# Two heads at a time in the second layer's attention, and a feed-forward's second product by Strassen's scheme

## The chip, the cores and the metric

The kernel runs on one core of one Trainium2 chip. The metric is the device time of one execution in microseconds; each version is run several times and the median is given. A separate, profiled execution gives the trace: for each instruction its engine, start, duration and what released it. Engine names in the rows: PE is TensorE's matrix multiply, PEld its weight load, DVE is VectorE, ACT is ScalarE, POOL is GpSimd and SP is SyncE, which only issues the DMAs here. All data is f32.

## The reference, cut to what matters

Two transformer blocks follow each other on 256 tokens of width 1024. The first (gated linear attention, retention and a mixture of 32 experts) is not touched. The second has a mixer of two attentions, then a cross-attention to a memory, then a feed-forward. What the change touches:

```
# mixer: 8 DSA heads and 8 NSA heads of width 64, 256 tokens, causal
idx = sum_h relu(q_i[h] @ k_i.T) * w_i[h]           # 8 index heads -> which 64 keys each query keeps
o_dsa[h] = softmax(q_d[h] @ k_d.T on the 64 kept keys) @ v_d            # one k, v for all 8 heads
o_cmp[h] = softmax(q_n[h] @ k_c[g].T) @ v_c[g]      # 15 compressed keys, g = h // 4
o_slc[h] = softmax(q_n[h] @ k_slc[g].T) @ v_slc[g]
o_win[h] = softmax(q_n[h] @ k_win[g].T) @ v_win[g]
o_nsa[h] = o_cmp * gate[h, 0] + o_slc * gate[h, 1] + o_win * gate[h, 2]
x = x + concat(o_dsa, o_nsa) @ w_out
...
x = x + square(relu(rms_norm(x) @ w_ff_in)) @ w_ff_out      # 1024 -> 4096 -> 1024
```

With 256 tokens the selection of blocks and the window reach over all earlier keys, so that both are plain causal attention here. The kernel thus has 24 attentions of one head (8 selected, 8 window, 8 DSA), and the eight small ones on 15 compressed keys.

## The kernel before

One program per engine, written out by hand; the engines meet at semaphores that count upwards, and each engine does its instructions in the order written. SyncE streams the weights as tiles of 1 MB through a ring of six (`RING`); a tile's slot is loaded again when the matmuls that read it have signalled. PSUM has eight banks of 128x512 f32. Banks 0 to 3 take the planned sums (`SUMS`, handed out in turn by `fresh`, taken by ScalarE with `take` or `copy`); banks 4 to 7 are used by hand. Queries are held turned (features by tokens) and two heads to a tile of 128 rows: the even head in rows 0 to 63, the odd one in 64 to 127; the keys stand doubled in both halves. `RT(q)` is such a pair tile.

The stage around the change, in TensorE's order:

- Index scores: for each of eight heads `causal_scores` (lines 1660 and 1661) into bank 4 or 5. It makes two matmuls, queries 0 to 127 against keys 0 to 127, and queries 128 to 255 against all 256 keys, 384 columns in all. ScalarE takes the relu (line 1032), VectorE adds it up with the head's weight (line 2411).
- Compressed scores (line 1675) for both halves, first all even heads, then all odd ones. VectorE masks them, ScalarE takes the exponential, VectorE sums. TensorE transposes the result (line 1684, `cp0` to `cp3`) and multiplies by the compressed values (line 1690, `co0`, `co1`). ScalarE copies the two banks out, VectorE divides by the sum and multiplies by the gate (line 2444) and so begins `OA`, the output by tokens.
- The loop over 24 heads. In turn n TensorE makes the scores of head n (one of banks 4 and 5), the three transposes of the probabilities of head n-2 (line 1718, banks 6 and 7), and the value product of head n-3 (lines 1729 to 1731), in which the turned probabilities are the weights and the 64 columns of V move. VectorE adds the mask (line 2477) and takes the two maxima (line 2487). In the first 16 turns it also does one step of the search for the 64 best keys, eight at a time on one row tile (lines 2483 and 2493). ScalarE takes the exponentials with their sums (line 1053), copies the turned probabilities (line 1062), and after each four heads copies the output bank (line 1070). VectorE's `finish` then divides by the sums, multiplies by the gate and adds into `OA` (lines 2454 to 2466).
- After the loop `OA` is transposed (`aT0` to `aT3`, line 1188) into `oT2`, and the output projection `ao0` to `ao3` runs (line 1179).

The feed-forward at the end: 16 tiles `ff0` to `ff15` (line 1170) with relu by ScalarE and the square by VectorE (line 2557), giving `ffh`, 32 blocks of 128 features by 256 tokens. Then 16 tiles of 256 x 1024 weights: for each, two row tiles of tokens, two halves of 512 output columns and two blocks of 128 features, 128 matmuls of 512 columns in all (line 1822), added up in banks 4 to 7. When the first two banks are complete (`tile0_done`) VectorE adds them to the residual with a factor per token (line 2562); the other two follow at the end, and SyncE stores the output by row tile (line 566).

## Time and profile before

| | |
|---|---|
| median of 3 runs | 1346.31 us (1344.46 to 1349.18) |
| profiled execution | 1351.78 us, with a span of 1350.0 us from first to last instruction |
| TensorE busy (matmul) | 1277.1 us, 95% of the span |
| VectorE busy | 289.7 us, 21% |
| ScalarE busy | 334.2 us, 25% |
| mean granted TensorE clock | 0.938 of full speed |
| feed-forward's second half | 110.0 us of matmul busy time on line 1822 |

The busy shares are of the whole span; stages differ, and the rows further down are read by stage. A record of the trace is one instruction. An f32 matmul and its weight load appear as two records each, a transpose as one. The duration of a matmul record includes the time in which it is in the pipeline together with the next, so that the cost of one matmul in a series is the distance from start to start. In a merged row (x8) the time runs from the first start to the last end. The granted clock has two levels, 1.00 (2.4 GHz) and 0.50 (1.2 GHz); a value between them is a stretch with both.

### The profile page before, as it was taken

How to read it: one execution, taken by the hardware profiler on the slowest of the kernel's cores; microseconds unless marked ns; L12 is line 12 of the kernel's file. 1: busy time of each engine (PE TensorE's matmuls, PEld its weight loads, DVE VectorE, ACT ScalarE, POOL GpSimd, SP SyncE). 2: the span in 40 equal slices, each digit the busy share in tenths (PEclk: the TensorE clock that was granted, in tenths of full speed). 3: DMA queues.
4: the chain of work that ended last, by engine and by line, in shares of the span. 5: the costliest groups of instructions: out<-in, count | busy, mean ns of one | idle time of the engine just before them, and what ended most of it. 6: DMA issues, size and time to landing. Idle time of an engine off the chain costs nothing.

```text
span 1350.0 us, 16638 instructions
## 1 busy us (share of the span) xinstructions
PE 1277.1 (95%) x6964; PEld 958.0 (71%) x6964; DVE 289.7 (21%) x757; ACT 334.2 (25%) x728; POOL 20.3 (2%) x26
## 2 busy tenths in 40 slices
PE   6899999999999899999999998967999979999998
PEld 5688888888887688865555556756677857887443
DVE  1200000012322211311111112683552121000000
ACT  3375100053322400321112213223333241000000
POOL 0000000000000000000000001020000000000000
PEclk9999999999999899899999999985555989999999
DMA  9921122213256954569999965430000413444430
GB/s 365 415 96 63 65 92 94 94 63 121 98 218 254 372 184 147 212 248 408 420 418 424 420 276 219 152 103 28 1 0 1 132 56 127 154 156 156 156 125 31
DMA packets 34362, 241.66 MB, mean 179 GB/s; under 512 B 3898, under 2 KB 4282, under 8 KB 6012
## 3 DMA queue, kind: packets, MB, share of 16 engines
q1 hardware_dynamic: 32640, 233.85, 45.1%
q10 hardware_dynamic: 1020, 4.02, 0.8%
q0 software_dynamic: 640, 2.90, 0.6%
q8 instruction: 46, 0.75, 0.2%
q14 instruction: 16, 0.13, 0.0%
HBM read 239.71 MB, written 1.05 MB: 178 GB/s over the span
## 4 chain that ended last, share of the span: by engine, by line
PE 88%; DVE 6%; ACT 2%; DMA 2%; issue 1%; SPq 0%; DVEq 0%; ACTq 0%
PE bank L1179 21%; PE bank L1170 20%; PE bank L1531 8%; PE bank L1822 8%; PE bank L1554 4%; PE bank L1493 3%; PE bank L1502 2%; DMA ring<-in_stream 2%; PE bank L1209 2%; PE bank L1661 1%; PE bank L1660 1%; PE bank L1229 1%; PE bank L1796 1%; PE bank L1406 1%; PE bank L1351 1%
## 5 line engine op out<-in xcount | busy, mean ns | idle before, releaser
L1170 PE MATMUL bank<-arena,ring 128*128 128x256 f32 x736 | 159.3, 379 | 0.0
L1170 PEld LDWEIGHTS bank<-arena,ring 128*128 128x128 f32 x736 | 139.8, 190 | 19.0
L623 ACT ACTIVATE arena<-bank 128x512 f32<-128x512 f32 x96 | 56.8, 597 | 340.1 <-PE bank L1170 211.3
L1179 PE MATMUL bank<-ring,arena 128*128 128x256 f32 x544 | 123.0, 387 | 7.3 <-DMA ring<-in_stream 4.4
L1179 PEld LDWEIGHTS bank<-ring,arena 128*128 128x128 f32 x544 | 105.0, 194 | 23.0 <-DMA ring<-in_stream 4.9
L1179 PE MATMUL bank<-ring,hTl 128*128 128x256 f32 x512 | 113.4, 380 | 0.0
L1170 PE MATMUL bank<-hTl,ring 128*128 128x256 f32 x512 | 112.6, 379 | 0.0
L1822 PE MATMUL bank<-ring,arena 128*128 128x512 f32 x256 | 110.0, 592 | 0.0
L1170 PEld LDWEIGHTS bank<-hTl,ring 128*128 128x128 f32 x512 | 97.0, 190 | 16.1 <-issue 3.4
L1179 PEld LDWEIGHTS bank<-ring,hTl 128*128 128x128 f32 x512 | 96.9, 190 | 15.2 <-issue 2.3
L1822 PEld LDWEIGHTS bank<-ring,arena 128*128 128x128 f32 x256 | 48.6, 190 | 60.8 <-issue 60.7
L1179 PE MATMUL bank<-ring,hTc 128*128 128x256 f32 x384 | 84.8, 379 | 0.0
L1179 PEld LDWEIGHTS bank<-ring,hTc 128*128 128x128 f32 x384 | 72.9, 190 | 11.7 <-issue 1.9
L1531 PE MATMUL bank<-ring,arena 128*64 128x256 f32 x512 | 57.0, 381 | 0.0
L1531 PEld LDWEIGHTS bank<-ring,arena 128*64 128x64 f32 x512 | 36.1, 137 | 24.0 <-issue 6.7
L2209 DVE TENSOR_TENSOR arena<-bank,arena 128x512 f32<-128x512 f32 x32 | 22.1, 692 | 101.9 <-PE bank L1554 101.9
L926 ACT ACTIVATE arena<-bank 128x256 f32<-128x256 f32 x16 | 6.1, 384 | 151.7 <-PE bank L1531 151.7
L912 ACT ACTIVATE arena<-bank,mod 128x256 f32<-128x256 f32 x72 | 36.5, 561 | 19.8 <-PE bank L1493 19.8
L1493 PE MATMUL bank<-arena 128*128 128x128 f32 x288 | 39.5, 281 | 1.4 <-DVE arena L2173 1.2
L1493 PEld LDWEIGHTS bank<-arena 128*128 128x128 f32 x288 | 34.8, 191 | 7.9 <-issue 7.5
L1502 PE MATMUL bank<-arena 64*128 64x512 f32 x136 | 33.8, 615 | 0.8 <-DVE arena L2209 0.8
L1053 ACT ACTIVATE arena<-arena,smx 128x128 f32<-128x128 f32 (+1 forms) x48 | 21.4, 447 | 52.4 <-DVE smx L2487 36.6
(445 smaller groups left out, 1462.6 us busy)
## 6 DMA issues: line engine op xcount, KB each, us to landing
ring<-in_stream SPq DMA_DIRECT2D x163, 1024.0 KB, 5.4
arena<-in_stream SPq DMA_DIRECT2D x38, 1024.0 KB, 9.1
hTl<-in_stream SPq DMA_DIRECT2D x9, 1024.0 KB, 8.2
hTc<-in_stream SPq DMA_DIRECT2D x9, 1024.0 KB, 10.1
consts<-in_consts ACTq DMA_DIRECT2D x1, 2665.0 KB, 13.3
arena<-in_mem SPq DMA_DIRECT2D x1, 1024.0 KB, 8.3
arena<-in_x SPq DMA_DIRECT2D x1, 1024.0 KB, 23.9
arena<-in_ctx SPq DMA_DIRECT2D x1, 1024.0 KB, 27.2
```

Of the source, the lines that this page charges most:

```text
L623: act.activation(dst, b[:, :].rearrange("p (a b) -> p a b", b=two), func, scale=scale).then_inc(sum_taken, 1)
L912: ins = act.activation(xgs[q][:, k, :].rearrange("p (e j c) -> p j e c", e=4, j=NT), b[:, 256 * m:256 * m + 256].rearrange("p (j e c) -> p ...
L1053: act.activation(sS[n % 3][:, a:z], sS[n % 3][:, a:z], ACT.Exp, bias=smx[:, 2 * (n % 4) + i:2 * (n % 4) + i + 1], accum_out=sm[:, i, hh:hh ...
L1170: mm = pe.matmul(b[:, 256 * n:256 * n + 256], w[:, k, 128 * n:128 * n + 128], h[:, k, :], start=(k == 0), stop=(k == KD - 1))
L1179: mm = pe.matmul(b[:, 256 * i:256 * i + 256], h[:, k, 128 * i:128 * i + 128], w[:, k, :], start=(k == 0), stop=(k == KD - 1))
L1209: mm = pe.matmul(b[:, 256 * i:256 * i + 256], h[:, k, 128 * i:128 * i + 128], w[:, k, :], start=(k == 0 and i == 0), stop=(k == KD - 1), s ...
L1493: mm = pe.matmul(bank[1 + fill % 2][:, at:at + 128], xn2[:, j, 128 * k:128 * k + 128], Pm[:, j, :], start=True, stop=True)
L1502: mm = pe.matmul(acc[2 * j + n][:, :], hT_PT[own, 256:384], ysb[own, 512 * n:512 * n + 512], start=False, stop=False, skip_group_check=True)
L1531: mm = pe.matmul(bank[0][CAP * e:CAP * e + CAP, FF * a:FF * a + FF], xgs[q][:, k, at:at + CAP], w[e][:, k, :], start=(k == 0), stop=(k == ...
L1554: mm = pe.matmul(bank[1 + m][to:to + CT, :], hT_PT[:, of:of + CT], wd[e][:, k, 512 * m:512 * m + 512], start=(k == 0), stop=(k == 1), skip ...
L1822: mm = pe.matmul(acc[2 * j + n][:, :], ffh[:, 2 * q + k, 128 * j:128 * j + 128], w[:, k, 512 * n:512 * n + 512], start=(q == 0 and k == 0) ...
L2209: dve.tensor_tensor(ysb[:, 512 * m:512 * m + 512], bank[1 + m][:, :], g2bc[:, 512 * m:512 * m + 512], ALU.mult).then_inc(R.y_taken, 1)
```

## The change

**Attention, two heads in a step.** The 24 turns become 12 steps (`STEPS`): eight for the NSA heads (`pair_step` alternates the selected and the window attention of one pair), four for the DSA pairs.

- `pair_of_scores` issues the two heads' matmuls alternately, even head from rows 0 to 63 into one bank, odd head from rows 64 to 127 into the next. The index scores use it too.
- VectorE adds the mask and takes the negated maximum in one `tensor_tensor_reduce` per head and row tile, four in a step. It does both row tiles' top-8 search and replacement in each of the first eight steps. It scales the probabilities by one over their sum and by the gate (`pair_norm`) before they are transposed; `finish` and `OA` are gone.
- The value product is turned round: V (keys by 64) is the weight, and the turned probabilities move, 256 columns for the first key block and 128 for the second. The even head writes partitions 0 to 63 of a bank, the odd one 64 to 127. Selected, window and compressed parts are added up in the same bank, and the result is `oT2` as it stands; four copies by ScalarE take it out. The transposes `aT0` to `aT3` and the sums `co0`, `co1` are gone.
- The compressed scores come ahead of the index scores and alternate the row halves; their softmax runs among the index heads and scales before the transposes. The product with the compressed values is eight matmuls in column tiles at step 2.

**Feed-forward's end by Strassen.** Each tile of 256 x 1024 weights is read as a 2x2 matrix of blocks (128 features by 512 columns), the activations likewise (128 features by 128 tokens). Seven products per tile, each with a bank of its own over all 16 tiles, take the place of eight. VectorE makes the sums of the activations (`fsum`, after each square) and of the weights (`wsum`, two buffers). At the end the seven banks go into the four quarters of the residual in twelve updates (`contribute`).

The core of the diff:

```diff
-            for h in range(H2):
-                if h >= 2:
-                    pe.wait_ge(idx_relu, h - 1)
-                causal_scores(bank[4 + h % 2], 8 + h // 2, 17, h % 2).then_inc(idx_ready, 1)
+            def pair_of_scores(at, qpair, kpair, ready):
+                for i, (a, z) in enumerate(TILES):
+                    for half in range(2):
+                        r = slice(64 * half, 64 * half + 64)
+                        mm = pe.matmul(bank[at + half][:, a:z], RT(qpair)[r, 128 * i:128 * i + 128],
+                                       RT(kpair)[r, 0:z - a], start=True, stop=True)
+                        if i == 1:
+                            mm.then_inc(ready, 1)
...
+            for p in range(4):
+                if p == 1:
+                    pe.wait_ge(cs_sub, 1)
+                elif p >= 2:
+                    pe.wait_ge(idx_relu, 2 * p - 2)
+                pair_of_scores(4 + 2 * (p % 2), 8 + p, 17, idx_ready)
+            pe.wait_ge(cs_norm, 1)
...
+            for s in range(STEPS + 3):
+                if s < STEPS:
+                    q, k, _ = pair_step(s)
+                    if s >= 2:
+                        pe.wait_ge(s_max, s - 1)
+                    else:
+                        pe.wait_ge(idx_relu, 6 + 2 * s)
+                    pair_of_scores(4 + 2 * (s % 2), q, k, s_ready)
+                if s == 2:
+                    pe.wait_ge(sum_taken, NO["cp3"] + 1)
+                    for p in range(4):
+                        for half in range(2):
+                            h = 2 * p + half
+                            pe.matmul(bank[p // 2][64 * half:64 * half + 64, 256 * (p % 2):256 * (p % 2) + 256],
+                                      VC[0:NCMP, p // 2, :], PCT[0:NCMP, 2 * h:2 * h + 2, :],
+                                      start=(p % 2 == 0), stop=False, skip_group_check=True)
+                m = s - 2
+                if 0 <= m < STEPS:
+                    pe.wait_ge(pair_norm, m + 1)
+                    for half in range(2):
+                        if m >= 1:
+                            pe.wait_ge(pt_taken, 2 * m + half - 1)
+                        for c in range(3):
+                            mm = pe.transpose(bank[2 + half][:, 128 * c:128 * c + 128], sS[m % 3][:, half, 128 * c:128 * c + 128], ident)
+                        mm.then_inc(pt_ready, 1)
+                m = s - 3
...
-                    mm = pe.matmul(b[:, HD * hh:HD * hh + HD], T[:, 0:128], v(0), start=True, stop=True)
-                    pe.matmul(b[:, 256 + HD * hh:256 + HD * hh + HD], T[:, 128:256], v(0), start=True, stop=False)
-                    mm = pe.matmul(b[:, 256 + HD * hh:256 + HD * hh + HD], T[:, 256:384], v(1), start=False, stop=True)
-                    mm.then_inc(av_done, 1)
-            pe.wait_ge(o_taken, 7)
-            for k in range(4):
-                turn(f"aT{k}", OA, k)
+                    for k in range(2):
+                        for half in range(2):
+                            last = k == 1 and (m % 2 == 1 or m >= H2)
+                            mm = pe.matmul(b[64 * half:64 * half + 64, at + 128 * k:at + 256], v(k),
+                                           pT[m % 2][:, half, 256 * k:256 * k + 256 - 128 * k],
+                                           start=(m in (8, 10) and k == 0), stop=last, skip_group_check=True)
...
-                S(dve.tensor_tensor(sS[n % 3], bank[4 + n % 2][:, 0:384], mask, ALU.add))
...
-                for i, (a, z) in enumerate(((0, 128), (128, 384))):
-                    dve.tensor_reduce(smx[:, 2 * (n % 4) + i:2 * (n % 4) + i + 1], sS[n % 3][:, a:z], AX.X, ALU.max,
-                                      negate=True).then_inc((dve_step, s_max)[i], 1)
...
+                    for half in range(2):
+                        for i, (a, z) in enumerate(TILES):
+                            ins = dve.tensor_tensor_reduce(sS[s % 3][:, half, a:z], bank[4 + 2 * (s % 2) + half][:, a:z], mask[:, a:z],
+                                                           -1.0, 3e38, ALU.add, ALU.min,
+                                                           nmax[:, s % 2, 2 * half + i:2 * half + i + 1])
+                    ins.then_inc(s_max, 1)
...
+                m = s - 1
+                if m >= 0:
+                    dve.wait_ge(probs, m + 1)
+                    W(dve.reciprocal(pair_sum[:, m % 2, :], pair_sum[:, m % 2, :]))
+                    for half in range(2):
+                        for i, (a, z) in enumerate(TILES):
+                            r = pair_sum[:, m % 2, 2 * half + i:2 * half + i + 1]
+                            pr = sS[m % 3][:, half, a:z]
+                            if m < H2:
+                                h = 2 * (m // 2) + half
+                                ins = dve.tensor_scalar(pr, pr, r, gates[:, i, h, 1 + m % 2:2 + m % 2], ALU.mult, ALU.mult)
+                            else:
+                                ins = dve.tensor_scalar(pr, pr, r, None, ALU.mult)
+                    ins.then_inc(pair_norm, 1)
...
-                for j in range(NT):
-                    for n in range(2):
-                        for k in range(2):
-                            mm = pe.matmul(acc[2 * j + n][:, :], ffh[:, 2 * q + k, 128 * j:128 * j + 128],
-                                           w[:, k, 512 * n:512 * n + 512], start=(q == 0 and k == 0), stop=(q == 15 and k == 1))
+                pe.wait_ge(fsum_ready, q + 1)
+                product(2, rows_sum[:, 128:256], w[:, 0, 0:512])
+                product(5, rows_sum[:, 0:128], w[:, 1, 512:1024])
+                if q == 0:
+                    pe.wait_ge(sum_taken, len(SUMS))
+                pe.wait_ge(wsum_ready, q + 1)
+                product(3, f0[:, 0:128], w3)
+                product(4, f1[:, 128:256], w4)
+                product(1, diag, w1)
+                product(7, across, w67[:, 1, :])
+                mm = pe.matmul(prod[6][:, :], down, w67[:, 0, :], start=(q == 0), stop=(q == 15))
                 mm.then_inc(ffo_done, 1)
...
+            def weight_sums(q):
...
+                if q >= 2:
+                    dve.wait_ge(ffo_done, q - 1)
+                dve.tensor_tensor(w3, w[:, 0, 512:1024], w[:, 1, 512:1024], ALU.subtract)
+                dve.tensor_tensor(w4, w[:, 1, 0:512], w[:, 0, 0:512], ALU.subtract)
+                dve.tensor_tensor(w1, w[:, 0, 0:512], w[:, 1, 512:1024], ALU.add)
+                dve.tensor_tensor(w67, w[:, :, 0:512], w[:, :, 512:1024], ALU.add).then_inc(wsum_ready, 1)
```

## Rows read from the trace of the kernel before

**Rows 1.** The page: clock over 40 slices of the span, and the chain by engine.

```profile
PEclk9999999999999899899999999985555989999999
...
PE 88%; DVE 6%; ACT 2%; DMA 2%; issue 1%; SPq 0%; DVEq 0%; ACTq 0%
```

**Rows 2.** Stretches: start and end, length, busy PE, PEld, DVE, ACT, POOL, clock, DMA.

```profile
945.00:1037.00 92.00, 85.63 (x309) 65.38 (x308) 48.32 (x154) 35.73 (x126) 0.00 (x0) 0.50 0.00 1
...
1235.00:1346.00 111.00, 110.52 (x260) 48.87 (x258) 2.54 (x4) 0.60 (x1) 0.00 (x0) 1.00 0.30 109
```

**Rows 3.** Timeline of one head: start us, us, engine, line, operation.

```profile
976.40 0.79 PE L1660 MATMUL bank<-hTc,hTl 64*128 64x128 f32 x2
...
977.98 0.90 PE L1718 MATMUL bank<-consts,arena 128*128 128x128 f32 x3
978.08 0.56 DVE L2477 TENSOR_TENSOR arena<-bank,consts 128x384 f32<-128x384 f32 x1 [2.82 <-PE bank L1661]
...
978.67 0.52 PE L1729 MATMUL bank<-arena 128*128 128x64 f32 x2
...
978.88 0.61 DVE L2487 TENSOR_REDUCE smx<-arena 128x1 f32<-128x128 f32 x2
...
979.98 0.79 PE L1660 MATMUL bank<-hTc,hTl 64*128 64x128 f32 x2
```

**Rows 4.** Timeline of the loop's start, heads 0 and 1 together.

```profile
944.18 0.81 PE L1660 MATMUL bank<-hTc,hTl 64*128 64x128 f32 x4 [0.69 <-ACT arena L1043]
...
945.86 0.56 DVE L2477 TENSOR_TENSOR arena<-bank,consts 128x384 f32<-128x384 f32 x1 [0.63 <-PE bank L1661]
```

**Rows 5.** Timeline of the experts' stage, TensorE, where matmuls use parts of the array.

```profile
652.28 3.64 PE L1554 MATMUL bank<-arena 128*32 128x512 f32 x32
655.85 7.13 PE L1531 MATMUL bank<-ring,arena 128*64 128x256 f32 x64
...
664.00 1.99 PE L1502 MATMUL bank<-arena 64*128 64x512 f32 x8
```

**Rows 6.** Groups of instructions by shape: count, busy us, mean ns of one, idle before.

```profile
L2557 DVE TENSOR_TENSOR arena<-arena 128x512 f32<-128x512 f32 x16 | 11.1, 693 | 94.8 <-ACT arena L623 94.8
...
L1053 ACT ACTIVATION_READ_ACCUMULATOR arena<-arena,smx 128x1 f32 x48 | 9.0, 187 | 0.0
...
L2483 DVE MAX8 top<-arena 128x8 f32<-128x256 f32 x8 | 3.3, 417 | 0.0
...
L2493 DVE MATCH_REPLACE8 arena<-top,arena 128x256 f32<-128x256 f32 x8 | 3.3, 409 | 0.0
...
L2009 DVE TENSOR_SCALAR arena<-arena,hv 128x256 f32<-128x256 f32 x8 | 2.8, 348 | 0.0
...
L2282 DVE TENSOR_SCALAR arena<-arena,mv,hms 128x64 f32<-128x64 f32 x2 | 0.6, 312 | 0.0
```

**Rows 7.** Timeline ahead of the loop: index scores, compressed scores and their product.

```profile
916.02 0.50 PE L1660 MATMUL bank<-arena,hTc 64*128 64x128 f32 x4
...
922.98 6.33 PEld L1675 LDWEIGHTS bank<-arena,hTl 64*128 64x128 f32 x32
...
936.41 7.09 PE L1690 MATMUL bank<-arena 15*128 15x64 f32 x32 [0.68 <-ACT arena L1038]
```

**Rows 8.** After the loop: timeline, then stretches with busy PE, clock and DMA.

```profile
1036.92 3.47 PE L1188 MATMUL bank<-consts,arena 128*128 128x128 f32 x16 [1.91 <-DVE arena L2466]
...
1041.07 11.28 PE L1179 MATMUL bank<-ring,arena 128*128 128x256 f32 x51 [0.69 <-ACT arena L623]
...
1039.00:1040.00 1.00, 1.00 (x7) 0.50 0.00 0
1040.00:1041.00 1.00, 0.39 (x3) 0.98 0.00 0
```

**Rows 9.** The feed-forward's second half: its group on the page, and its last updates.

```profile
L1822 PE MATMUL bank<-ring,arena 128*128 128x512 f32 x256 | 110.0, 592 | 0.0
...
1345.56 1.41 DVE L2562 SCALAR_TENSOR_TENSOR arena<-bank,r,arena 128x512 f32<-128x512 f32 x2 [2.02 <-PE bank L1822]
```

More of the change, by code:

```diff
@@ L217, in plan @@
     sums.extend(f"cp{n}" for n in range(4))
-    sums.extend(["co0", "co1"])
-    sums.extend(f"aT{k}" for k in range(4))
     for j in range(4):
@@ L2402, in _, with idx_added @@
             dve.wait_ge(kc_ready, 1)
-            for h in range(H2):
+            dve.wait_ge(heads_ready, 4)
+            dve.wait_ge(cs_ready, 2)
+            c16 = cS.rearrange("p (g n) -> p g n", n=16)[:, :, 0:NCMP]
+            cm = C("cmask").rearrange("p (i n) -> p i n", i=NT)
+            for par in range(2):
+                for i in range(NT):
+                    at = 8 * par + 4 * i
+                    S(dve.tensor_tensor(c16[:, at:at + 4, :],
+                                        bank[6 + par][:, 64 * i:64 * i + 64].rearrange("p (h n) -> p h n", n=16)[:, :, 0:NCMP],
+                                        cm[:, i, :].unsqueeze(1).broadcast_to([P, 4, NCMP]), ALU.add))
+                    step.one()
+            dve.wait_ge(dve_step, step.n)
+            W(dve.tensor_reduce(cmx, c16, AX.X, ALU.max))
+            W(dve.tensor_scalar(cmx, cmx, -BIG / 10, None, ALU.max))
+            dve.tensor_tensor(c16, c16, cmx.unsqueeze(2).broadcast_to([P, 16, NCMP]), ALU.subtract).then_inc(cs_sub, 1)
+            def idx_added(h):
                 dve.wait_ge(idx_relu, h + 1)
-                for i, (a, z) in enumerate(((0, 128), (128, 384))):
+                for i, (a, z) in enumerate(TILES):
                     w = wsc[:, i, h:h + 1]
@@ L2417, in _ @@
                         dve.wait_ge(idx_taken, h + 1)
[L2418 to L2432 removed]
+            for h in range(2):
+                idx_added(h)
             dve.wait_ge(cs_exp, 1)
@@ new lines, in _ @@
+                S(dve.tensor_tensor(c4[:, par, :, :], c4[:, par, :, :], gates[:, :, par:8:2, 0], ALU.mult))
+                step.one()
+            dve.wait_ge(dve_step, step.n)
+            dve.tensor_tensor(c16, c16, crs.unsqueeze(2).broadcast_to([P, 16, NCMP]), ALU.mult).then_inc(cs_norm, 1)
+            for h in range(2, H2):
+                idx_added(h)
+            W(dve.tensor_tensor(iacc, iacc, C("causal"), ALU.add))
+            for s in range(STEPS + 1):
+                if s < STEPS:
+                    dve.wait_ge(s_ready, 2 * s + 2)
+                    if s >= 3:
+                        dve.wait_ge(pt_ready, 2 * s - 4)
+                    mask = C("causal") if s < H2 else ibias
+                    for half in range(2):
+                        for i, (a, z) in enumerate(TILES):
+                            ins = dve.tensor_tensor_reduce(sS[s % 3][:, half, a:z], bank[4 + 2 * (s % 2) + half][:, a:z], mask[:, a:z],
+                                                           -1.0, 3e38, ALU.add, ALU.min,
+                                                           nmax[:, s % 2, 2 * half + i:2 * half + i + 1])
+                    ins.then_inc(s_max, 1)
+                if s < H2:
+                    for i, (a, z) in enumerate(TILES):
+                        S(dve.max(top8[:, 8 * i:8 * i + 8], iacc[:, a:z]))
+                        step.one()
+                    dve.wait_ge(dve_step, step.n)
+                    for i, (a, z) in enumerate(TILES):
+                        S(dve.match_replace(iacc[:, a:z], top8[:, 8 * i:8 * i + 8], iacc[:, a:z], -3e38))
+                        step.one()
+                    dve.wait_ge(dve_step, step.n)
+                if s == H2 - 1:
```

309 lines of the change are left out of this document (131 added, 178 removed).

## The prediction, made before the changed kernel was run

> **What bounds the kernel now.** I read the page's second part and its chain first. The chain that ends last is 88% TensorE, so a microsecond of TensorE work on it is a microsecond of time, and the clock row has one long trough, at 5 of 10 (the lower level, 1.2 GHz, against 2.4), between slices 27 and 31 [rows 1]. The table of stretches puts the trough on the attention: from 945 to 1037 us TensorE is busy 85.6 of 92 us, VectorE 48.3, ScalarE 35.7, and the granted clock is 0.50 throughout. The second half of the feed-forward (from 1235) is at 1.00, with VectorE almost idle (2.5 of 111 us) [rows 2]. So both edited stages are bound by TensorE, the first at the lower clock, and each has idle VectorE time to spend.
>
> The attention's period is read from one head: its score matmuls start at 976.40 and the next head's at 979.98, so 3.58 us for a head [rows 3]. An f32 matmul is two records. At this clock a 256-column one takes 0.85 us and a 128-column one 0.43: 1.28 for the scores. Three transposes are 0.64 (977.98 to 978.67, with a 0.05 handover). The three value matmuls stream only 64 columns each but load 128 columns of weights twice, six loads at 0.21, 1.28. These are 3.20; the other 0.38 is the two changes between the 64-row and the 128-row array shape, each about 0.2. Twenty-four heads are 86 us.
>
> **The change, part by part.** Times below are positions in the span of the profiled run.
>
> *Scores in row tiles.* The trace of before already holds the case by accident. One head's scores, issued at 976.40, reach VectorE at 978.08, 1.68 us later [rows 3]. Heads 0 and 1, which stand in different halves of the rows and in different banks, are issued together at 944.18, all eight records have started by the time VectorE starts on them at 945.86, again 1.68 us [rows 4]. The MoE's row-tiled L1502 agrees: eight 512-column records in 1.99 us, where one at a time would be 8 x 0.43 = 3.4 [rows 5]. So two heads' scores cost 1.28 us, not 2.56.
>
> *Value product turned round, in column tiles.* V (64 columns) becomes the weights and the probabilities move: per head one matmul of 256 columns and one of 128, 1.28 us at this clock; two heads use the two column halves. The MoE runs just this shape: L1531, 128x64 weights and 256 columns, 64 records in 7.13 us, 0.11 each, where L1822's rate (512 columns in 0.43) gives 0.215 for one alone; and four 32-column tiles (L1554) are four times as fast [rows 5, 9]. I take full overlap: 1.28 for two heads, the upper bound being 2.56. The six transposes stay, 1.28. The array changes shape three times in a step (rows, full, columns), 0.57.
>
> Here the Trainium skill speaks against the change: "TensorEngine Tiling (Array Packing)", section Tiling Modes, says that a change of tiling mode drains TensorE. The trace agrees, as the 0.38 us per head above; by rule and row alike the three changes are in my sum already.
>
> TensorE's step of two heads is then 1.28 + 1.28 + 1.28 + 0.57 = 4.4 us at the lower clock, against 7.16 before.
>
> *VectorE's step* becomes nearly as long. Before, per head: mask add 0.56, two maxima 0.61 together [rows 3]. Now four tensor_tensor_reduce do both, of 128 and 256 columns from two banks. No row shows one; the nearest is a tensor_tensor (0.69 for 512 columns, 0.56 for 384, so about 0.21 and 0.34 from start to start): 1.2 us. If each also needs a separate read of its accumulator, as ScalarE's 0.19 us ones, it is 2.0 [rows 6]; below 1.2 it can't go, as every column still passes once. In the first eight steps both top-8 searches and replacements follow (0.42 and 0.41 for 256 columns, some two thirds of that for 128; 1.5 us with their loads and waits). The division by the sum, formerly on the finished output, now scales the probabilities: a reciprocal and four tensor_scalar with one or two scalars per row, between 0.31 (two scalars, 64 columns) and 0.35 (one scalar, 256 columns) each, with waits 1.5 us [rows 6]. Together 4.3 us (upper bound 5.3) for steps 0 to 7, 2.8 to 3.6 for 8 to 11. ScalarE was busy 35.7 us for 24 heads less three [rows 2], some 1.5 a head, and does the same work in a step for two: 3.0.
>
> How they interlock: transposes of step s-2 wait for VectorE's scaling at the end of its step s-1; then TensorE goes through transposes, values and the scores of s+1 (4.5 us with handovers) before VectorE can begin s+1. The two overlap except for that 4.5, so I take 4.6 for steps 0 to 7 and 4.4 after.
>
> *Ahead of the loop.* Before: index scores from 916.0, block scores to 929.6 (L1675, 32 records at 0.2, weight-load bound), softmax, transposes, L1690 (sixteen matmuls, 7.1 us, no cover), first head scores at 944.18 [rows 7, 4]. Now the block scores come first and alternate row halves (3.2 to 6.3 us; I take 4.5, as no row shows two 128-column loads in different halves by themselves): done by 920.5. The softmax chain on VectorE runs beside the index pairs; cs_norm comes at about 926, the transposes end at 929.5, VectorE, the last in this part, adds index heads 2 to 7 (0.8 each with waits, an estimate from the 0.56 of one 384-column operation) until 931.5 and starts step 0 there. TensorE already has its scores. L1690 becomes eight column-tiled matmuls of 256 columns (3.4 us) that TensorE runs at step 2 while it waits for the first scaling (at 939): covered; without that cover they cost 3.4.
>
> *The loop.* Step 0 (no scaling) ends 934.2; seven at 4.6: 966.4; the index bias, 1.0: 967.4. Then TensorE sets the end: scores 9 finished at 971.9, two more steps 980.7, and the drain (three groups of transposes, four of values, one copy) 11.3: the output projection starts at 992.0. Before it was 1041.07 [rows 8]. What also goes: the last division and the sixteen turning transposes, since the product comes out already turned. Attention: 49.1 us less.
>
> *Clock after it.* Before, the clock rose at about 1040, after the transposes of L1188 had run back to back since 1036.92, so the projection began at 1.00 [rows 8]. Now it may begin at 0.50: some 4 us of it at half speed cost 2. Add 2.0.
>
> *Feed-forward by Strassen.* Per 256x1024 weight tile seven 512-column products instead of eight. 128 matmuls have 256 records at 0.43, 0.857 us for one [rows 9]; sixteen go: -13.7. VectorE makes the sums of the weights: per tile five 512-column adds, 5 x 0.69 = 3.5 us at most, beside 6.0 us of TensorE; with two buffers this stays hidden (without cover it would cost up to 3.5 x 16 = 56). The activation sums, some 1.3 us per tile, stand beside the first half's 6.9 us per tile (16 matmuls of 0.43). The first weight sum is made before the last tile of the first half; the second is ready 5.7 us after it, and needed at 7.7.
>
> The end grows. Before, VectorE has two updates after the last matmul, 1345.56 to 1346.97 [rows 9]. Now twelve updates of 0.7 follow seven products; the first can start 5.1 us before the last product ends, so they end 3.5 us behind it instead of 1.6: +1.9, and the first half of the output leaves almost with the second instead of 3.4 us ahead: +0.9. Together +2.8.
>
> **Sum.** -49.1 + 2.0 - 13.7 + 2.8 = -58.0 us. Against the profiled run's 1351.78 that is 1293.8. The median of the runs shown, 1346.31, is 5.5 lower; the same difference off it gives **1288.3**.
>
> **The rivals.** (a) *The clock rises inside the loop.* For: a step now holds more streaming per microsecond (3.84 of 4.6 us against 2.56 of 3.58), and the clock has risen upon transposes alone [rows 8]. Against: it stayed at 0.50 through a stage in which TensorE was 93% busy [rows 2]. The first eight steps, then bound by VectorE's 4.3, hardly gain; the last four fall from 4.4 to about 3.2 and the drain halves: 7 to 8 us, and the 2.0 goes: 1279. The Trainium skill, "TensorE: Matmul & The Clock Gate", section Part 4: PE-mode transpose, says that transposes don't count as activity for the clock. By that rule the step would have 2.56 us of activity in 4.6, less than before, and this rival falls. The trace disagrees: only transposes ran before 1040. (b) *VectorE sets the step*: the fused operation needs its accumulator read, 5.3 to 5.5 us for steps 0 to 7 and some wait in the others: +7 to +10, 1297. (c) *The tiles don't overlap or Strassen is not covered*: value products one after the other, +1.28 x 12 = 15; or the seven products wait for sums. Against: rows 5. About 1304. (d) *Slower than before*: the fused reduction in VectorE is so dear that it eats all. The other savings are worth some 58 us, so a step would have to take 58/12 = 4.8 us more, 9.4 in all, which is 6.3 for four instructions, 1.6 each, over four times the nearest row. Above that the kernel is slower, 1355 for 1.7 us each. (e) *It doesn't do what it says*: nothing in the diff leaves the old loop in place, so this is in (c).
>
> **Chances.** Forecast 0.42, (a) 0.27, (b) 0.18, (c) 0.10, (d) 0.02, 0.01 left. The forecast's own range is 1283 to 1294 (block scores, handovers, the bound of the copies). With (a) and (b): 1276 to 1302. 0.3% is about what a measurement of this kernel can tell from no change: faster 0.97, same 0.01, slower 0.02.
>
> **What the profile would show.** Right: the output projection (L1179's arena records) starts near 992; start to start of pair scores 4.6 us in the first eight steps, 4.4 in the last four; the score records of both halves in pairs; the feed-forward's second half 112 matmuls in 96 us; seven products 6.0 us apart; 3.5 us of VectorE after the last. Wrong: tensor_tensor_reduce rows over 0.45 us or with a second record (b); a granted clock of 1.00 between 931 and 990 (a); value records at 0.43 each for 256 columns (c); idle TensorE between products, released by VectorE's weight sums (c).

## The result and the profile after

The changed kernel takes 1276.93 us (median of 4 runs, 1275.76 to 1280.01) against 1346.32, a ratio of 0.9486 with a 95% interval of 0.9462 to 0.9511: 69.4 us less, where 58.0 were forecast. The time lies at the lower end of the range given (1276 to 1302) and outside the forecast's own 1283 to 1294. It is nearest to rival (a), 1279, and 11.4 us below the forecast of 1288.3.

The page of the changed kernel: the clock row and the chain, as in [rows 1].

```profile
PEclk9999999999999999999999999899778989999999
...
PE 85%; DVE 7%; ACT 2%; DMA 2%; SPq 2%; issue 1%; DVEq 0%; ACTq 0%
```

The long trough of 5s is gone. Two slices at 7 are left where the attention now stands.

The two profiled runs differ by 76.0 us of span (1350.0 and 1274.0), more than the medians. In four pieces:

| piece | before | after | difference | forecast |
|---|---|---|---|---|
| up to the compressed keys (L1652, now L1665) | 915.8 | 910.8 | -5.0 | 0 |
| from there to the output projection (L1179, now L1192) | 125.3 | 65.9 | -59.4 | -49.1 |
| from there to the last product's first matmul | 194.4 | 194.3 | -0.1 | +2.0 |
| feed-forward's second half to the span's end | 114.5 | 103.0 | -11.5 | -10.9 |

The first piece has no edit in it. Over the fourteen profiled runs of this document it lies between 910.6 and 915.8 us, so its 5.0 us are scatter, with the profile of before at the top (its 1351.78 against a median of 1346.31 said so already). The edits are worth 71 us in the profiles. Of the attention's 59.4, 16.4 are saved ahead of the loop (30.1 to 13.7 us) and 43.0 from its start to the output projection (95.2 to 52.2).

Timeline of the changed kernel from the compressed keys to the loop (start us, us, engine, line, operation), to be held against [rows 7]. CUSTOM_DVE_ANT_0 is how the trace names the tensor_tensor_reduce:

```profile
910.84 0.29 PE L1665 MATMUL bank<-consts,arena 15*128 15x15 f32 x2 [2.35 <-DVE ss L2426]
911.50 1.74 PE L1687 MATMUL bank<-arena,hTl 64*128 64x15 f32 x22 [0.38 <-ACT arena L1042]
...
914.09 1.68 PE L1675 MATMUL bank<-arena,hTc 64*128 64x128 f32 x8
...
919.87 1.92 PE L1703 MATMUL bank<-consts,arena 128*15 128x128 f32 x16
...
924.53 0.29 DVE L2485 CUSTOM_DVE_ANT_0 arena<-bank,consts 128x128 f32<-128x128 f32 x1
...
927.15 3.67 PE L1718 MATMUL bank<-arena 15*64 15x256 f32 x16
```

The loop's first VectorE instruction comes 13.7 us after the compressed keys; before it was 30.1 (915.8 to 945.86 in [rows 4]). The compressed scores (L1687) are through in 2.6 us, where [rows 7] have 6.3. While the clock is at 0.50, two of their records, one in each row half, take 0.21 us together; before, each took 0.21.

Timeline of one step at each clock, the lower first:

```profile
935.07 1.54 PE L1728 MATMUL bank<-consts,arena 128*128 128x128 f32 x6 [0.79 <-DVE arena L2511]
...
936.54 1.55 PE L1742 MATMUL bank<-arena 128*64 128x256 f32 x8
...
938.02 1.65 PE L1675 MATMUL bank<-hTc,hTl 64*128 64x128 f32 x8
...
939.75 0.29 DVE L2485 CUSTOM_DVE_ANT_0 arena<-bank,consts 128x128 f32<-128x128 f32 x1 [0.81 <-PE bank L1675]
...
947.59 0.28 DVE L2485 CUSTOM_DVE_ANT_0 arena<-bank,consts 128x128 f32<-128x128 f32 x1
947.73 0.88 PE L1728 MATMUL bank<-consts,arena 128*128 128x128 f32 x6 [1.39 <-DVE arena L2511]
...
948.36 0.42 DVE L2485 CUSTOM_DVE_ANT_0 arena<-bank,consts 128x256 f32<-128x256 f32 x1
948.54 0.87 PE L1742 MATMUL bank<-arena 128*64 128x256 f32 x8
948.70 0.08 DVE L2485 DVE_READ_ACCUMULATOR2_ANT arena<- 128x1 f32 x1
948.70 0.61 DVE L2491 MAX8 top<-arena 128x8 f32<-128x128 f32 x2
...
949.34 0.93 PE L1675 MATMUL bank<-arena,hTl 64*128 64x128 f32 x8
...
950.13 0.18 DVE L2504 RECIPROCAL arena<-arena 128x4 f32<-128x4 f32 x1
950.35 1.25 DVE L2511 TENSOR_SCALAR arena<-arena 128x128 f32<-128x128 f32 x4
...
951.51 0.28 DVE L2485 CUSTOM_DVE_ANT_0 arena<-bank,consts 128x128 f32<-128x128 f32 x1
```

At 0.50 the six transposes, the four value matmuls and the four score matmuls start 1.47 and 1.48 us apart, and VectorE gets the scores 1.73 us after their start: 4.7 us, and VectorE waits 0.81 for them. At 1.00 the same three take 2.5 us, TensorE stands idle 1.39 us until VectorE has scaled the probabilities, and VectorE doesn't wait at all: its own 3.92 us (947.59 to 951.51) are the period. The reducing instruction costs what a tensor_tensor does (0.42 us for 256 columns out of a bank, as line 2206 of the kernel before: 0.421); its accumulator read is a record of 0.08 us within the distance to the next.

Stretches of the changed kernel: start and end, length, busy PE, clock, DMA.

```profile
939.90:956.00 16.10, 9.86 (x88) 1.00 0.00 0
956.90:960.40 3.50, 3.50 (x21) 0.53 0.00 0
960.70:970.00 9.30, 6.58 (x58) 1.00 0.01 2
970.70:973.70 3.00, 3.00 (x15) 0.50 0.00 0
```

The clock is low from 926 to 939.7, high for most of what follows, and falls twice, each time after TensorE had stood idle (2.38 us before 956.6, 2.04 us before 970.5). That a gap of this length always brings a fall is not shown: `one_buffer`, further down, has the same attention code and a gap of 2.05 us at the second place, and there the clock stayed at 1.00. The end of the feed-forward, as in [rows 9]:

```profile
1262.18 8.19 DVE L2600 SCALAR_TENSOR_TENSOR arena<-bank,r,arena 128x512 f32<-128x512 f32 x12 [3.76 <-PE bank L1835]
...
1266.27 1.02 PE L1850 MATMUL bank<-hTl,arena 128*128 128x512 f32 x2
1269.74 1.00 SPq L583 DMA_DIRECT2D out<-arena  x2
```

The seven products of 16 tiles run from 1171.0 to 1267.1, 96.1 us, and VectorE's twelve updates end 3.2 us behind.

### The profile page after: what moved, and what is told of

Read it like the earlier page. It is cut to its first block, busy times and chain, and to the rows that moved or that the text cites. A ratio compares the mean times of both kernels' runs of the same rounds, so it can differ in the third digit from the quotient of the medians.

```text
span 1274.0 us, 16580 instructions
## 1 busy us (share of the span) xinstructions
PE 1198.1 (94%) x6852; PEld 893.8 (70%) x6852; DVE 350.8 (28%) x944; ACT 327.9 (26%) x720; POOL 20.3 (2%) x26
## 4 chain that ended last, share of the span: by engine, by line
PE 85%; DVE 7%; ACT 2%; DMA 2%; SPq 2%; issue 1%; DVEq 0%; ACTq 0%
PE bank L1192 22%; PE bank L1183 21%; PE bank L1544 9%; PE bank L1835 6%; PE bank L1567 4%; PE bank L1506 3%; PE bank L1515 3%; DMA arena<-in_stream 2%; PE bank L1222 2%; PE bank L1242 1%; PE bank L1807 1%; PE bank L1419 1%; PE bank L1416 1%; PE bank L1364 1%; PE bank L1850 1%
## 5 line engine op out<-in xcount | busy, mean ns | idle before, releaser
L640 ACT ACTIVATE arena<-bank 128x512 f32<-128x512 f32 x92 | 54.2, 597 | 336.6 <-PE bank L1183 211.3
L1192 PE MATMUL bank<-ring,arena 128*128 128x256 f32 x544 | 119.7, 380 | 3.8 <-DVE arena L2059 2.2
L1192 PEld LDWEIGHTS bank<-ring,arena 128*128 128x128 f32 x544 | 102.6, 190 | 18.5 <-DVE arena L2059 2.6
L1192 PE MATMUL bank<-ring,hTl 128*128 128x256 f32 x512 | 113.4, 380 | 0.0
L1192 PEld LDWEIGHTS bank<-ring,hTl 128*128 128x128 f32 x512 | 96.9, 190 | 15.2 <-issue 2.3
L1192 PE MATMUL bank<-ring,hTc 128*128 128x256 f32 x384 | 84.8, 379 | 0.0
L1192 PEld LDWEIGHTS bank<-ring,hTc 128*128 128x128 f32 x384 | 72.9, 190 | 11.7 <-issue 1.9
L1948 DVE TENSOR_TENSOR arena<-arena 128x512 f32<-128x512 f32 x12 | 7.6, 688 | 102.5 <-ACT arena L801 102.5
L2231 DVE TENSOR_TENSOR arena<-arena,bank 128x256 f32<-128x256 f32 x16 | 6.7, 421 | 101.3 <-ACT arena L943 101.3
L1222 PE MATMUL bank<-ring,arena 128*128 128x256 f32 x128 | 32.2, 409 | 0.6 <-ACT arena L677 0.6
```

Of the source, the lines that this page charges most:

```text
L640: act.activation(dst, b[:, :].rearrange("p (a b) -> p a b", b=two), func, scale=scale).then_inc(sum_taken, 1)
L1192: mm = pe.matmul(b[:, 256 * i:256 * i + 256], h[:, k, 128 * i:128 * i + 128], w[:, k, :], start=(k == 0), stop=(k == KD - 1))
L1222: mm = pe.matmul(b[:, 256 * i:256 * i + 256], h[:, k, 128 * i:128 * i + 128], w[:, k, :], start=(k == 0 and i == 0), stop=(k == KD - 1), s ...
```

## The experiments

My theory after the result: once the clock is up, VectorE's 3.92 us set the first eight steps; TensorE's part of a step, and thus the overlap of the tiles, counts only ahead of the loop, while the clock is low and in the last steps; Strassen is additive and rests on hidden sums. The rival: TensorE's round of work and waits sets the period, as in my forecast. "Loop" below is the time from the first tensor_tensor_reduce to the output projection, 52.2 us in the changed kernel.

**The parts one by one.** Each kernel has one half of the change, the other half as before. "That chip" and "the same chip" mean that both kernels of a comparison ran on one chip. `attn_only` keeps the new attention and has the old last product back:

```diff
-                product(2, rows_sum[:, 128:256], w[:, 0, 0:512])
-                product(5, rows_sum[:, 0:128], w[:, 1, 512:1024])
...
+                for j in range(NT):
+                    for n in range(2):
+                        for k in range(2):
+                            mm = pe.matmul(acc[2 * j + n][:, :], ffh[:, 2 * q + k, 128 * j:128 * j + 128],
+                                           w[:, k, 512 * n:512 * n + 512], start=(q == 0 and k == 0), stop=(q == 15 and k == 1))
```

> The changed kernel with the feed-forward's second half as it was before (eight products per tile, in banks 4 to 7). Theory (the two parts add up): Strassen was worth 11.5 us in the profiles (114.5 us from the first matmul of that half to the end before, 103.0 after), so the median is 1276.9 + 11.5 = 1288.4. Rival (the weight sums on VectorE cost something elsewhere that this takes back too): under 1285.

Measured: 1286.68 us, 0.9543 (0.9528 to 0.9559) of before's 1347.74 on that chip, -61.1 us.

> The kernel before with Strassen's scheme alone. Theory (parts add up): 1346.3 - 11.5 = 1334.8. Rival (the gain needs the new attention, for instance because the feed-forward begins at another clock): over 1338.

Measured: 1337.37 us, 0.9919 (0.9902 to 0.9935), -10.4 us. Its edit is the attention part of the change taken back, Strassen kept. The sum, -71.4, is the whole change within its intervals (-69.4 in one comparison, -72.1 in another). The parts add up, and neither needs the other. In the profiles each has exactly its piece: the feed-forward's end takes 103.0 us in `ff_only` and 114.5 in `attn_only`.

**The tiles forced apart.** In `scores_apart` and `values_apart` TensorE waits for its own even head before it issues the odd one.

```diff
-                for i, (a, z) in enumerate(TILES):
-                    for half in range(2):
+                for half in range(2):
+                    if half == 1:
+                        pe.wait_ge(ready, 2 * n + 1)
+                    for i, (a, z) in enumerate(TILES):
```

> The changed kernel, but the odd head's scores wait until the even head's are finished, so the two row tiles never run together; index scores too. Theory (VectorE sets the first eight steps once the clock is at 1.00, with 1.4 us of idle TensorE in each step of 3.92): the 0.6 us more per step is hidden there, and only the four steps at 0.50, the index scores and the last steps pay, some 4 us: 1281. Rival (TensorE sets the step, as my forecast had it at the low clock): 1.3 us in each of 12 steps and in 4 index pairs, 20 us: 1297.

Measured: 1283.07 us, 0.9529 (0.9509 to 0.9549), some 6 us more than the changed kernel, where I expected 4. The trace says where: 17.9 us ahead of the loop instead of 13.7 (the index pairs), and a loop of 53.5 instead of 52.2. In the steps at 1.00 the period stays 3.92 (945.41, 949.34, 953.26, 957.18 are the starts of four).

```diff
-                    for k in range(2):
-                        for half in range(2):
+                    for half in range(2):
+                        if half == 1:
+                            pe.wait_ge(av_done, 2 * m + 1)
+                        for k in range(2):
```

> The changed kernel, but the odd head's value product waits until the even head's is finished, so the two column tiles never run together. Theory (VectorE sets the first eight steps): hidden where the clock is at 1.00, 0.7 us more in each of the last steps and 1.3 us in those at the low clock: 5 us, 1282. Rival (TensorE sets the step): 1.3 us in each of 12 steps, 15 us: 1292.

Measured: 1281.09 us, 0.9509 (0.9493 to 0.9525); its interval touches the changed kernel's. The median is some 4 us above the changed kernel's, near the 5 expected, but in the trace (of the fastest of its four executions, 1277.45) the part from the compressed keys to the projection is only 1.8 us longer, 1.5 of it in the loop, with the same 3.92 in the steps at 1.00. The other 2 us have no place in the trace; unedited stretches scatter by as much. Why the loop pays so little is told by the stretches. Those of `values_apart` (columns: length, busy PE, PEld, DVE, ACT, POOL, clock, DMA):

```profile
940.00:957.00 17.00, 13.86 (x92) 8.36 (x88) 16.07 (x78) 10.92 (x41) 0.00 (x0) 1.00 0.00 1
957.00:975.00 18.00, 16.06 (x101) 10.21 (x102) 10.72 (x58) 12.12 (x45) 0.00 (x0) 1.00 0.01 2
```

The longer value products leave no long gap, and the clock stays at 1.00 to the end, where the changed kernel has 0.82 from 957 to 975. Part of what the apart tiles cost in work they seem to get back in clock; no run separates the two. The rival (1297 and 1292) is out.

**VectorE's work taken away and added.** `no_search` leaves out the search for the 64 best keys inside the loop (its mask is then another one, the last steps' work the same); `unfused` makes mask and maximum by separate instructions again.

```diff
-                if s < H2:
-                    for i, (a, z) in enumerate(TILES):
-                        S(dve.max(top8[:, 8 * i:8 * i + 8], iacc[:, a:z]))
...
-                        S(dve.match_replace(iacc[:, a:z], top8[:, 8 * i:8 * i + 8], iacc[:, a:z], -3e38))
```

> The changed kernel without VectorE's search for the 64 best keys inside the first eight steps (top-8 and replacement left out, 1.45 of its 3.92 us per step; the last four steps then use another mask, with the same work). Theory (VectorE sets those steps): the period falls from 3.92 to about 3.1, where ScalarE's 3.0 us are next, 0.8 x 7 = 5 to 6 us less: 1271. Rival (something else sets the 3.92, for instance the round of waits between the engines): no change, 1277.

Measured: 1266.63 us, 0.9389 (0.9373 to 0.9404). The loop is 42.4 us, 9.8 shorter, more than the 5 to 6 expected: 6.5 of it from the first step to the ninth. The steps from 938.21 to 959.31 are alternately 2.5 and 3.7 us apart, 3.0 on average. ScalarE, busy 15.3 of 17 us, is probably next; that wasn't tested. The stretches show that the clock did not fall again, which gives the rest.

```profile
940.00:957.00 17.00, 13.39 (x121) 8.70 (x117) 14.15 (x71) 15.28 (x59) 0.00 (x0) 1.00 0.01 1
957.00:975.00 18.00, 15.24 (x106) 11.73 (x105) 5.66 (x32) 9.82 (x29) 0.00 (x0) 1.00 0.01 1
```

```diff
-                            ins = dve.tensor_tensor_reduce(sS[s % 3][:, half, a:z], bank[4 + 2 * (s % 2) + half][:, a:z], mask[:, a:z],
-                                                           -1.0, 3e38, ALU.add, ALU.min,
-                                                           nmax[:, s % 2, 2 * half + i:2 * half + i + 1])
+                        S(dve.tensor_tensor(sS[s % 3][:, half, :], bank[4 + 2 * (s % 2) + half][:, 0:384], mask, ALU.add))
...
+                            ins = dve.tensor_reduce(nmax[:, s % 2, 2 * half + i:2 * half + i + 1], sS[s % 3][:, half, a:z],
+                                                    AX.X, ALU.max, negate=True)
```

> The changed kernel, but mask and maximum again by two kinds of instruction as before (one add of 384 columns per head, two maxima), instead of tensor_tensor_reduce. Theory (VectorE sets the first eight steps): 2.3 us instead of 1.2 per step, so a period of 5.0 instead of 3.9 there, 8 to 9 us, and 1 to 2 in the last four steps: 1287 to 1289. Rival (TensorE's round sets the period): under 1281.

Measured: 1286.96 us against 1277.62 for the changed kernel on the same chip (`after_again` below), 9.3 more, as expected. The period is 4.90 us in the steps in which it was 3.92, and the loop is 61.2. Timeline, from one step's first add to the next step's:

```profile
945.36 1.01 DVE L2484 TENSOR_TENSOR arena<-bank,consts 128x384 f32<-128x384 f32 x2
...
950.26 1.02 DVE L2484 TENSOR_TENSOR arena<-bank,consts 128x384 f32<-128x384 f32 x2
```

VectorE's instructions set the period in both directions; the one-instruction form is worth 9 us of the change by itself.

**One buffer for the weight sums.** The sums of a tile wait for the tile before, and TensorE for them.

```diff
-                w67, w1, w3, w4 = wsum[q % 2]
+                w67, w1, w3, w4 = wsum[0]
...
-                if q >= 2:
-                    dve.wait_ge(ffo_done, q - 1)
+                if q >= 1:
+                    dve.wait_ge(ffo_done, q)
```

> The changed kernel with one buffer for the sums of the weights instead of two, so that VectorE begins a tile's sums only when the seven products of the tile before are done. Theory (Strassen's gain rests on these sums being hidden): of 3.1 us from the last product to the sums' end, the first two products of the next tile cover 1.7; 1.4 us of idle TensorE for each of 15 tiles, 21 us: 1298, more than Strassen brings. Rival (the sums lie elsewhere off the path): under 1282.

Measured: 1304.40 us, 0.9673 (0.9655 to 0.9692), some 27 us more than with two. Timeline of two tiles:

```profile
1192.85 0.69 DVE L2574 TENSOR_TENSOR arena<-ring 128x512 f32<-128x512 f32 x1 [4.72 <-PE bank L1850]
...
1194.66 1.22 DVE L2577 TENSOR_TENSOR arena<-ring 128x1024 f32<-128x1024 f32 x1
1195.94 3.70 PE L1835 MATMUL bank<-arena 128*128 128x512 f32 x8 [1.48 <-DVE arena L2577]
```

TensorE stands 1.48 us per tile for the sums. In the whole trace a tile takes 7.75 us from start to start instead of 6.01, and the feed-forward's end is 26.6 us longer. So the price is 1.74 us per tile for 15 tiles, where I had taken 1.4. Strassen saves 0.86 per tile; without the second buffer it loses.

**The clock.** In `filler` TensorE's idle time is filled with transposes of the identity that nothing reads, into columns 384 to 511 of a score bank that VectorE has finished with.

```diff
+                if {5: 10, 6: 10, 7: 10, 8: 18, 12: 16}.get(s):
+                    pe.wait_ge(s_max, min(s, STEPS - 1))
+                    for c in range({5: 10, 6: 10, 7: 10, 8: 18, 12: 16}[s]):
+                        pe.transpose(bank[4 + 2 * ((s + 1) % 2) if s < STEPS else 4][:, 384:512], ident, ident)
```

> The changed kernel with transposes of the identity added in TensorE's idle time, into unused columns of a score bank that VectorE has finished with: 10 in each of steps 5 to 7, 18 after the scores of step 8, 16 at the start of the drain. Nothing reads them. Theory (the clock fell at 956 and at 970 because TensorE stood idle for some 2 us before, and transposes count as work for it): the clock stays at 1.00 from 940 to the output projection, and the pieces at 0.50 (957 to 960.5 and 970.5 to 974) shrink: 3 us less, 1274. Rival, by what the Trainium skill says in 'TensorE: Matmul & The Clock Gate', Part 4 (a transpose doesn't count as activity): the clock falls as before and the median is 1277 or more.

Measured: 1274.96 us, 0.9446 (0.9430 to 0.9462); the interval touches the changed kernel's, so the trace decides. Its timeline at the places where the clock had fallen (L1724 is the filler):

```profile
958.15 2.18 PE L1724 MATMUL bank<-consts 128*128 128x128 f32 x18
960.60 0.88 PE L1732 MATMUL bank<-consts,arena 128*128 128x128 f32 x6 [0.26 <-DVE arena L2515]
...
971.83 1.97 PE L1724 MATMUL bank<-consts 128*128 128x128 f32 x16
973.63 0.82 PE L1732 MATMUL bank<-consts,arena 128*128 128x128 f32 x6
```

And its stretches there (busy PE, clock, DMA share, GB/s):

```profile
959.00:960.00 1.00, 1.00 (x12) 1.00 0.00 0
...
973.00:974.00 1.00, 1.00 (x12) 1.00 0.00 0
```

The clock stays at 1.00 from 944 to the projection, and the loop is 49.7 us instead of 52.2. Transposes keep the clock up here: the first fall is in every trace with a gap of 1.8 to 2.4 us ahead of step 8's transposes (the changed kernel twice, `attn_only`, `one_buffer`, `pool_eight`) and in none in which the filler takes the gap's place. The second fall is a weaker witness, as it is missing from `one_buffer` (loop 50.6 us) and `pool_eight` too, which have no filler. The Trainium skill ("TensorE: Matmul & The Clock Gate", section Part 4: PE-mode transpose) says that the fast clock doesn't engage for transposes, since they don't count as busy in the same way. This trace of f32 transposes disagrees, and it decides.

**A faster version.** `pool_eight` gives GpSimd, idle in the loop, the scaling of the odd head in the first eight steps; `pool_filler` adds the filler (7, 7, 7, 16 and 16 transposes); `pool_filler_early` adds 9 more after the scores of step 1.

```diff
+            for m in range(H2):
+                pool.wait_ge(recip_ready, m + 1)
+                for i, (a, z) in enumerate(((0, 128), (128, 384))):
+                    r = pair_sum[:, m % 2, 2 + i:3 + i]
+                    pr = sS[m % 3][:, 1, a:z]
...
+                        ins = pool.tensor_scalar(pr, pr, r, gates[:, i, h, 1 + m % 2:2 + m % 2], ALU.mult, ALU.mult)
```

> The changed kernel, but in the first eight steps GpSimd, idle otherwise, scales the odd head's probabilities, VectorE only the even head's. Theory (VectorE sets the step): its step falls from 3.92 to 3.3 us, 7 x 0.6 = 4 us less: 1273. Rival (GpSimd is too slow or disturbs VectorE: one tensor_scalar of 1024 columns took it 2.84 us, so 0.36 and 0.71 us for 128 and 256 if it goes by columns, and more if each has a fixed cost): the transposes of the odd head come late and the median is 1277 to 1285.

Measured: 1273.53 us, 0.9443 (0.9425 to 0.9461). Timeline of one step:

```profile
945.34 0.73 DVE L2529 TENSOR_SCALAR arena<-arena 128x128 f32<-128x128 f32 x2
945.40 1.09 POOL L630 TENSOR_SCALAR arena<-arena 128x128 f32<-128x128 f32 x2 [2.30 <-DVE arena L2521]
...
945.99 0.27 DVE L2502 CUSTOM_DVE_ANT_0 arena<-bank,consts 128x128 f32<-128x128 f32 x1
946.19 0.91 PE L1745 MATMUL bank<-consts,arena 128*128 128x128 f32 x6 [0.83 <-DVE arena L2529]
...
949.39 0.27 DVE L2502 CUSTOM_DVE_ANT_0 arena<-bank,consts 128x128 f32<-128x128 f32 x1
```

GpSimd's two take 1.09 us beside VectorE's 0.73, and the period is 3.40, where I expected 3.3; the loop is 46.5. VectorE pays a little for its neighbour: its scaling of 256 columns takes 0.47 us beside GpSimd, against 0.41 in the changed kernel. The one of 128 columns stays at 0.35.

`after_again` is the changed kernel without an edit, on the chip of the two that follow and of `unfused`.

> The changed kernel as it is, on the same chip as the three others, so that they can be compared with it directly: 0.9486 of before, 1277 to 1279.

Measured: 1277.62 us, 0.9471 (0.9447 to 0.9496) of before's 1349.67.

> GpSimd scaling the odd heads in the first eight steps, and idle TensorE time filled with transposes of the identity (7 in steps 5 to 7, 16 after the scores of step 8, 16 at the start of the drain). Theory: both gains are of different places (VectorE's step; the pieces at 0.50 after step 8), so they add up: some 6 + 3 = 9 us less than the changed kernel, 1269. Rival: with shorter steps the clock stays up by itself, and the filler adds nothing: 1272.

Measured: 1270.67 us, 0.9411 (0.9389 to 0.9432) on the same chip, 7.0 us less than the changed kernel, the intervals apart. The loop (45.5) is only 1.0 shorter than with GpSimd alone, and the two intervals overlap, so that the filler's share is shown by the trace alone. The two gains overlap too: with GpSimd alone the clock fell only once, from 955 to 958.

The last one's addition to `pool_filler`:

```diff
+                if s == 1:
+                    pe.wait_ge(sum_taken, NO["cp3"] + 1)
+                    for c in range(9):
+                        pe.transpose(bank[2][:, 384:512], ident, ident)
```

> The same, with 9 more transposes in the gap after the scores of step 1, before the clock falls at 926. Theory: the product with the compressed values and steps 2 and 3 then run at 1.00; TensorE was late there by 0.8 us once, so 1 us less: 1268. Rival: the clock falls anyhow (not enough work in that stretch), or the transposes delay the scores of step 2: 1269 to 1270.

Measured: 1270.33 us, 0.9422 (0.9399 to 0.9445), the same. Its stretches of busy PE and clock:

```profile
926.00:928.00 2.00, 2.00 (x21) 1.00 0.03 8
928.00:930.00 2.00, 0.97 (x10) 0.95 0.00 0
930.00:932.00 2.00, 1.20 (x6) 0.50 0.00 0
```

It only moved the fall by some 4 us, to 930: the compressed product now ran at 1.00, was done sooner, and a gap of 1.8 us came after it.

What the experiments leave open is how the loop's 43.0 us divide. Row tiles, column tiles and the one-instruction form, each taken back by itself, cost 1.3, 1.5 and 9.0 us of loop. The value product turned round, the end of `finish` and `OA`, and the higher clock were not taken back, and no run has the new loop at 0.50 throughout.

## Why the prediction was right, and where it was not

The time fell as forecast, by 69.4 us for 58.0, and the tiles and Strassen's scheme worked as priced. The mechanism of the loop did not hold: the forecast had TensorE's round of work at the low clock set every step, and what set seven of the first eight was VectorE's work. The measured 1276.93 lies in the range by 0.9 us, and only because the range took in rival (a), whose chance was put at 0.27. For the loop, that is luck as much as insight.

*Row tiles, column tiles: right.* Scores, transposes and values at the lower clock take 1.73, 1.47 and 1.48 us with their handovers, 4.7 in all; the forecast's 4.4 to 4.5 plus the way to VectorE. What failed is which of them matters: with the clock up, the apart tiles cost nothing in the steps that VectorE sets.

*The step in 0 to 7: the period was mis-sized, 4.6 for 3.9, and put down to the wrong engine.* Two terms. VectorE's step was put at 4.3 and is 3.92: four tensor_tensor_reduce take 1.11 us for the 1.2 forecast, search and replacement 1.43 for 1.5, the scaling 1.38 for 1.5, as I had put waits on top of pipelined instructions. (The three forecast parts add up to 4.2, not 4.3.) And 4.6 was TensorE's figure at the low clock. It holds for one period (934.93 to 939.75, 4.82) and not for the others. Two of those, from 927.08 to 934.93, lie at 0.50 as well and are 3.92 and 3.93 us: TensorE had no value product to do there yet. So the clock is only one reason. First step to ninth: 31.9 us, forecast 35.9.

*The clock: the likeliest case was chosen wrongly.* I gave the low clock up to the projection 0.42 and the rise 0.27. My argument against the rise was that the clock had stayed at 0.50 with TensorE 93% busy. But that busy share [rows 2] belonged to the old loop's mix of work, not to the new one's; the rise upon transposes alone [rows 8] was the better witness. Why the old loop never got the higher clock, no run here shows. The count that left the transposes out was uneven too, as it did so for the new loop alone: without them it is 1.92 of 3.58 us before and 2.56 of 4.6 after, which is not less. From the ninth step to the projection: 20.3 us, forecast 24.6, and 17.8 in `filler`, which has neither fall. The 2.0 us for a projection that begins at 0.50 didn't come: it begins at 1.00.

*Ahead of the loop: right but 2.0 us dear.* The compressed scores were bounded by 3.2 and 6.3 us, I took 4.5, they took 2.6, below the lower bound: the 128-column loads of two row halves overlap in full (0.21 us for a pair at 0.50), and about half of the records ran at 1.00.

The first three terms make the difference in the attention, 2.0 + 4.0 + 4.3 = 10.3 of 59.4 against 49.1. The projection's 2.0 us are the next piece's, where nothing changed.

*Strassen: right.* 13.7 us of products and sums fully hidden (`one_buffer` shows by what). The end grew by 2.2 us (4.6 to 6.9 from the last product to the end) for 2.8.

*Rivals.* (b) came true by its name and not by its price: VectorE does set the step, but at 3.92 us and not at 5.3. The second record that was to be its sign is there, the accumulator read of 0.08 us, and adds nothing to the distance between instructions. (c) and (d) did not occur. (In (d), 1.7 us per instruction would by its own sum give some 1352, not 1355.) (a) did, in part: the clock rose at 939.7 and fell twice.

## What to carry to other kernels

When a change shrinks the work of the bounding engine by half, price the next engine's step instruction by instruction from start-to-start distances and not from durations plus waits: that engine may set the new period. Here its distances (1.11, 1.43 and 1.38 us) add up to the 3.92 that the step takes, where durations plus waits had given 4.3. In this kernel matmuls that use half of the array's rows or columns run in pairs for the price of one, but that pays only where TensorE is last; after that, each VectorE instruction fused away or given to GpSimd pays instead. Trading a product for sums on an idle engine paid here with two buffers for the sums (10.4 us less in `ff_only`); with one buffer the kernel took 27 us more than with two.

## What the runs showed of the hardware

- Two row-tiled weight loads of 128 columns overlap: a pair of records in the two row halves takes 0.21 us at 0.50, and so did a single one before. All 32 took 2.6 us, part of them at 1.00, where 32 one after the other took 6.3 at 0.50.
- A stretch of TensorE work spread over parts of the array with gaps of 1.4 us in 3.9 kept the clock at 1.00, while the old loop, 93% busy, never raised it; gaps of 2.38 us before 956.6 and of 2.04 us before 970.5 were followed by a fall. In `one_buffer`, with the same attention code, a gap of 2.05 us at the second place was not, and in `pool_eight` one of 1.84 us was not.
- With those gaps filled by transposes it stayed up (`filler`, 1.00 from 944 on), and in `values_apart`, whose longest gap after the rise is 1.46 us, it did so by itself.
- tensor_tensor_reduce is shown as a custom instruction of 0.28 and 0.42 us for 128 and 256 columns, with an accumulator read of 0.08 inside it. A tensor_tensor of 256 columns out of a bank takes 0.42 as well.
- A tensor_scalar of 256 columns on VectorE takes 0.47 us beside GpSimd's and 0.41 without; one of 128 columns takes 0.35 either way (`pool_eight`).
